# Two-layer diffusion trunk with expert-choice experts: last expert's rows added on the chip, another order in the ranking of layer 0, accumulated rows read in halves, and a hold on the expert weights

## What is computed

```python
def ec_moe(x, w_router, w_gate, w_up, w_down):
    cap = EC_CAPACITY * t // N_EXPERTS            # 64 latent rows, 16 context rows
    aff = jax.nn.softmax(logits, axis=1)
    gate, idx = lax.top_k(aff, cap)
    xs = jax.vmap(lambda xb, ib: xb[ib])(x, idx)
    hid = jax.nn.silu(xs @ w_gate) * (xs @ w_up)  # per expert, 1024 -> 512
    y = (hid @ w_down) * gate[..., None]          # per expert, 512 -> 1024
    return zeros.at[idx].add(y)

for layer in range(2):
    x = x + g1 * mixer(rms_norm(x, norm1) * (1 + sc1) + sh1)
    h = rms_norm(x, norm2) * (1 + sc2) + sh2
    x = x + g2 * ec_moe(h, ...)
y = rms_norm(x, final_norm)
```

## Time and profile before

| what | value |
|---|---|
| median of 3 runs | 1420.3 us (1416.61 to 1423.88) |
| the profiled execution | 1421.51 us, its span 1418.9 us |
| busy in the span: PE, PEld | 1264.6 us (89%), 916.2 us (65%) |
| busy: DVE, ACT, POOL | 872.5 us (61%), 734.3 us (52%), 215.8 us (15%) |
| DMA moved | 323.18 MB, mean 228 GB/s |
| chain that ended last | PE 71%, DMA 10%, DVE 9%, ACT 8%, issue 2% |
| mean granted TensorE clock | 0.945 of full |

### The profile page before, as it was taken

One profiled execution on the slowest core, in us unless ns is written; L12 is line 12 of the kernel. 1 busy time (PEld: TensorE's weight loads), 2 busy tenths in 40 slices (PEclk: granted clock), 3 DMA queues, 4 the chain that ended last, 5 costly groups with the idle time before them and its releaser, 6 DMA issues.

```text
span 1418.9 us, 18135 instructions
## 1 busy us (share of the span) xinstructions
PE 1264.6 (89%) x7524; PEld 916.2 (65%) x7524; DVE 872.5 (61%) x1005; ACT 734.3 (52%) x866; POOL 215.8 (15%) x126
## 2 busy tenths in 40 slices
PE   5899988898479999999689998999985899999991
PEld 3796756795256666666369994567954566666660
DVE  3713457424658888888274352454255699999993
ACT  3522137513547777778254114554145677777763
POOL 3000000020102222211120000000201033333320
PEclk9997799999889999999799999799998899999996
DMA  9721073004699999999793322002146999999985
GB/s 358 221 77 32 32 254 118 1 30 178 243 331 358 383 379 377 377 383 398 251 282 119 89 75 77 1 1 76 45 178 220 369 399 379 379 384 385 379 326 167
DMA packets 99047, 323.18 MB, mean 228 GB/s; under 512 B 6368, under 2 KB 30143, under 8 KB 82583
## 3 DMA queue, kind: packets, MB, share of 16 engines
q1 hardware_dynamic: 87360, 283.54, 53.2%
q0 software_dynamic: 9152, 30.53, 8.2%
q10 hardware_dynamic: 2454, 7.96, 1.5%
HBM read 298.20 MB, written 23.81 MB: 227 GB/s over the span
## 4 chain that ended last, share of the span: by engine, by line
PE 71%; DMA 10%; DVE 9%; ACT 8%; issue 2%; SPq 0%; ACTq 0%; DVEq 0%; POOLq 0%
PE psum L869 67%; ACT arena L1669 3%; DMA stage<-in_w_mod 2%; DVE arena L2119 2%; DVE w_lo L1841 2%; DMA arena<-in_moe_w_up 2%; DMA h_hi<-h_dram,arena 1%; DMA stage<-in_moe_w_gate 1%; DMA acc_dram<-arena 1%; PE psum L1349 1%; DMA arena<-acc_dram 1%; DVE arena L1879 1%; DMA arena<-in_ev_w_in 1%; DVE h_lo L1841 1%; ACT w_hi L1735 1%
## 5 line engine op out<-in xcount | busy, mean ns | idle before, releaser
L869 PE MATMUL psum<-w_hi,h_hi 128*80 128x512 f32 (+1 forms) x848 | 329.9, 389 | 12.5 <-DVE h_lo L1841 10.5
L1841 DVE TENSOR_TENSOR w_lo<-stage,w_hi 128x2048 fp32r<-128x2048 f32 (+1 forms) x120 | 270.9, 2270 | 89.6 <-ACT w_hi L1448 56.0
L869 PE MATMUL psum<-w_hi,h_lo 128*80 128x512 f32 (+1 forms) x848 | 325.9, 384 | 0.0
L869 PE MATMUL psum<-w_lo,h_hi 128*80 128x512 f32 (+1 forms) x848 | 325.7, 384 | 0.0
L869 PE MATMUL psum<-h_hi,w_hi 128*128 128x320 f32 x672 | 211.3, 314 | 6.9 <-DVE h_lo L1891 6.8
L1735 ACT ACTIVATE w_hi<-stage 128x2048 fp32r<-128x2048 f32 x98 | 186.7, 1915 | 44.3 <-PE psum L869 34.9
L869 PE MATMUL psum<-h_hi,w_lo 128*128 128x320 f32 x672 | 209.2, 311 | 0.0
L869 PE MATMUL psum<-h_lo,w_hi 128*128 128x320 f32 x672 | 209.2, 311 | 0.0
L1841 DVE TENSOR_TENSOR w_lo<-arena,w_hi 128x2048 fp32r<-128x2048 f32 x75 | 171.4, 2288 | 37.4 <-ACT w_hi L1735 36.9
L869 PEld LDWEIGHTS psum<-w_hi,h_hi 128*80 128x80 f32 (+1 forms) x848 | 129.8, 153 | 86.8 <-issue 14.8
L837 POOL DMA_INDIRECT acc_dram<-arena x32 | 120.6, 3770 | 427.2 <-ACT arena L1772 229.3
(11 more groups left out here) (236 smaller groups left out, 1296.0 us busy)
## 6 DMA issues: line engine op xcount, KB each, us to landing
stage<-in_w_mod SPq DMA_DIRECT2D x48, 1024.0 KB, 7.6
stage<-in_moe_w_up SPq DMA_DIRECT2D x35, 1024.0 KB, 14.7
stage<-in_moe_w_down SPq DMA_DIRECT2D x32, 1024.0 KB, 14.5
stage<-in_moe_w_gate SPq DMA_DIRECT2D x31, 1024.0 KB, 13.7
arena<-in_moe_w_gate SPq DMA_DIRECT2D x28, 1024.0 KB, 14.2
arena<-in_moe_w_up SPq DMA_DIRECT2D x24, 1024.0 KB, 15.3
arena<-in_moe_w_down SPq DMA_DIRECT2D x21, 1024.0 KB, 13.7
xT<-in_moe_w_down SPq DMA_DIRECT2D x11, 1024.0 KB, 19.5
```

What stands on the lines that cost most here:

```text
L869: return pe.matmul(o, w, x, start=first, stop=last, skip_group_check=True)
L1841: return nc.vector.tensor_tensor(dst, src, hi.bitcast(F32), ALU.subtract)
```

## The change

It has four parts.

1. **Hold.** In both layers SP waits, before the third weight block of the experts (expert 0's u0), until expert 0's rows are gathered. Before, this wait stood ahead of the eighth block in layer 0 and of the tenth in layer 1. One wait on the h stores is left out, since the gather implies it; the wait on the x stores in layer 1 stays.
2. **Ranked chunk first.** In layer 0 the `mod_rows` of the chunk of step "rank" moves ahead of the h transposes on PE, and its evacuation ahead of the h evacuations on ACT.
3. **Halves.** At the end of layer 0, ACT issues two reads (columns 0 to 511, 512 to 1023) in place of POOL's one; two of the four evacuations of step "acc" now stand behind that wait. PE transposes and DVE adds half by half.
4. **Last expert on the chip.** In layer 1, expert 15's rows aren't scattered. SP reads the tiles after expert 14's scatter. POOL counts 0 to 639 along 80 rows, DVE compares with the expert's token numbers, which makes an 80 x 640 one-hot matrix, and PE multiplies it (fp32, 10 matmuls of 512 columns) with the expert's rows. For tiles 0, 1 and 4 DVE adds the result to the tile read; for tiles 2 and 3, PE adds the tile in PSUM by four matmuls with the identity, and the norm works from PSUM. The tiles go in the order 0, 1, 4, 2, 3.

```diff
 def expert_piece(e, what):
...
+                    if m == 2:
+                        sp.wait_ge(gathered[0], 16 * (E // AHEAD * L + 1))
                     if m < SLOTS + len(lent_places):
...
                             filled(sp, (L, "h", NT - 1))
-                            if n in SUM_PLACES:
-                                sp.wait_ge(h_out[NT - 1], 16 * (L + 1))
-                            elif L == LAYERS - 1:
+                            if n in OUT_PLACES and L == LAYERS - 1:
                                 sp.wait_ge(x_stored, 16 * NT)
...
-            sp.wait_ge(scattered, 16 * E * LAYERS)
-            for t in range(NT):
-                sp.dma_start(acc_out[t], acc_dram[LAYERS - 1][P * t:P * t + P, :]).then_inc(acc_out_in[t], 16)
+            sp.wait_ge(scattered, 16 * (E * LAYERS - 1))
+            for t in TAIL_ORDER:
+                sp.dma_start(acc_last[t], acc_dram[LAYERS - 1][P * t:P * t + P, :]).then_inc(acc_out_in[t], 16)
...
 # pool
-                for e in range(E):
+                for e in range(E if L < LAYERS - 1 else E - 1):
...
-                pool.wait_ge(scattered, 16 * E * (L + 1))
-                if L < LAYERS - 1:
-                    pool.dma_start(xtok, acc_dram[L].rearrange("(t p) d -> p t d", p=P)).then_inc(acc_in, 16)
+                if L == LAYERS - 1:
+                    pool.wait_ge(lo_ready, moe_q[L] + piece_number(E - 1, "d0") + 1)
+                    pool.iota(one_hot, [[1, T]], base=0, channel_multiplier=0, allow_small_or_imprecise_dtypes=True).then_inc(token_numbers, 1)
...
 # tensor
+                if L == 0:
+                    mod_rows(ranked[0])
                 for t in range(NT):
...
+                if L == LAYERS - 1:
+                    pe.wait_ge(one_hot_ready, 1)
+                    pe.wait_ge(y_ready, n0 + E)
+                    for t in TAIL_ORDER:
+                        if t == 3:
+                            pe.wait_ge(x_added, 1)
...
+                            ins = mm(psum[:, TAIL_BANKS[t] + b, :], one_hot[rows, P * t:P * t + P], ysb[(E - 1) % 2][rows, cols_b],
+                                     True, t not in ADDED_BY_PE)
+                        if t in ADDED_BY_PE:
+                            pe.wait_ge(acc_out_in[t], 16)
+                            for b in range(2):
+                                ins = mm(psum[:, TAIL_BANKS[t] + b, :], ident, acc_last[t][:, FF * b:FF * b + FF], False, True)
...
-                    pe.wait_ge(acc_in, 16)
-                    to_features((L, "moe"), xtok)
+                    for b in range(2):
+                        pe.wait_ge(acc_in[b], 16)
...
 # scalar
-                    modulation("acc")
+                    modulation("acc", slice(0, 2))
+                    act.wait_ge(scattered, 16 * E * (L + 1))
+                    rows = acc_dram[L].rearrange("(t p) d -> p t d", p=P)
+                    for b in range(2):
+                        act.dma_start(xtok[:, :, FF * b:FF * b + FF], rows[:, :, FF * b:FF * b + FF]).then_inc(acc_in[b], 16)
+                    modulation("acc", slice(2, None))
...
 # vector
+                    nc.vector.tensor_scalar(one_hot, one_hot, last_slots, None, ALU.is_equal).then_inc(one_hot_ready, 1)
                 rows_out(E - 1)
...
+                nc.vector.tensor_tensor(x, psum[:, TAIL_BANKS[t]:TAIL_BANKS[t] + 2, :], x, ALU.add).then_inc(x_added, 1)
```

More of the change, by code:

```diff
@@ L267, in plan_psum @@
         p.add((L, "aff"), [4], "act"), p.add((L, "aff ctx"), [5], "act")
+        if L == 0:
+            p.add(("mod rows", ranked[0]), [6], "act")
         for t in range(NT):
@@ L271, in plan_psum @@
         for c in ranked:
-            p.add(("mod rows", c), [6], "act"), p.add(("mod turned", c), [6], "dve", in_order=False)
+            if L > 0:
+                p.add(("mod rows", c), [6], "act")
+            p.add(("mod turned", c), [6], "dve", in_order=False)
         for c in last:
@@ L287, in plan_psum @@
         mod("acc")
-        one((L, "moe", "ctx0"), "dve"), one((L, "moe", "ctx1"), "dve")
-        for k in range(KD):
-            one((L, "moe", k), "dve")
+        for b in range(2):
+            one((L, "moe", f"ctx{b}"), "dve")
+            for k in range(4 * b, 4 * b + 4):
+                one((L, "moe", k), "dve")
     return p
@@ L581, in trunk @@
         hid_step = sem("hid_step")
-        scattered, acc_in = sem("scattered"), sem("acc_in")
+        scattered, acc_in = sem("scattered"), [sem(f"acc_in{b}") for b in range(2)]
         dve_step = sem("dve_step")
+        token_numbers, one_hot_ready, last_added = (sem(n) for n in ("token_numbers", "one_hot_ready", "last_added"))
         def filled(eng, name):
@@ L662, in trunk, with summed_rows @@
         moe_q = [piece[(L, "moe", 0)]["q"] for L in range(LAYERS)]
+        def summed_rows(t):
+            if t not in ADDED_BY_PE:
+                return acc_last[t]
+            return psum[:, TAIL_BANKS[t]:TAIL_BANKS[t] + 2, :]
         block = ctx.enter_context(nc.Block())
@@ L1716, in _ @@
                 evacuate((L, "aff ctx"), work_ctx[:, 0:NC], bank((L, "aff ctx"))[CTX_ROW:RANKED, 0:NC])
+                if L == 0:
+                    modulation((L, "rank"))
                 for t in range(NT):
@@ L1816, in root_out_of @@
                 nc.scalar.activation(root_out[:, t:t + 1], root_out[:, t:t + 1], ACT.Exp, scale=-0.5).then_inc(root_done, 1)
-            for t in range(NT):
-                act.wait_ge(acc_out_in[t], 16)
-                nc.scalar.activation(x_out[t], acc_out[t], ACT.Square, accum_out=squares_out[:, t:t + 1]).then_inc(x_squared, 1)
-                if t:
-                    root_out_of(t - 1)
+            for n, t in enumerate(TAIL_ORDER):
+                if t in ADDED_BY_PE:
+                    act.wait_ge(last_added, n + 1)
+                else:
+                    act.wait_ge(x_added, n + 1)
+                src = summed_rows(t)
+                dst = y_rows[t].rearrange("p (b n) -> p b n", b=2) if t in ADDED_BY_PE else y_rows[t]
+                nc.scalar.activation(dst, src, ACT.Square, accum_out=squares_out[:, t:t + 1]).then_inc(x_squared, 1)
+                if n:
+                    root_out_of(n - 1)
             root_out_of(NT - 1)
@@ L2286, in _ @@
                 expert_split(E - 1, "d1")
+                if L == LAYERS - 1:
+                    then(nc.vector.tensor_copy(last_slots, slots[:, E - 1:E]))
+                    dve.wait_ge(token_numbers, 1)
+                    nc.vector.tensor_scalar(one_hot, one_hot, last_slots, None, ALU.is_equal).then_inc(one_hot_ready, 1)
                 rows_out(E - 1)
@@ L2299, in _ @@
                 newton(mean, root)
-                nc.vector.scalar_tensor_tensor(x_out[t], acc_out[t], root, gain_rows, ALU.mult, ALU.mult).then_inc(y_done, 1)
+                dst, gain = y_rows[t], gain_rows
+                if t in ADDED_BY_PE:
+                    dst, gain = (x.rearrange("p (b n) -> p b n", b=2) for x in (dst, gain))
+                    dve.wait_ge(last_added, n + 1)
+                nc.vector.scalar_tensor_tensor(dst, summed_rows(t), root, gain, ALU.mult, ALU.mult).then_inc(y_done, 1)
+            add_last(0)
+            add_last(1)
+            mean_of(0)
+            add_last(2)
+            mean_of(1)
+            scale_rows(0)
+            mean_of(2)
+            scale_rows(1)
+            mean_of(3)
+            scale_rows(2)
+            mean_of(4)
+            scale_rows(3)
+            scale_rows(4)
 _OUTS = {"y_prompt": (1, NC, D), "y_sample": (1, NL, D), "new_k": (1, 1, KV, NC, HD), "new_v": (1, 1, KV, NC, HD),
```

70 lines of the change are left out of this document (53 added, 17 removed).

## The result

The changed kernel takes 1431.4 us (median of 4 runs, 1429.6 to 1433.4) against 1419.9 before; the ratio is 1.0083, 95% interval 1.0065 to 1.0101. The forecast was 1414.6, with a range of 1405 to 1421. The profiled execution took 1432.5 us, its span is 1430.3.

What follows compares the result with a forecast made beforehand. PE and the weight stream's DMA are both full, so PE computes as fast as weights come. Layer 0's ranking +1.0, halves −2.0, layer 1's ranking +1.0, tail −5.7 sum to −5.7: median 1420.3 to 1414.6 us, range 1405 to 1421.

Steps and rivals of the forecast that it cites:

- by the row the matmuls start at 2.4 GHz and the tail gives −5.7: Tail: 14 fp32 matmuls at full clock take 12.2 us, PE resting only about 1.3 us before; −5.7 us.
- the rival of 1.2 GHz: Tail: its matmuls run at 1.2 GHz throughout, +6.5 in place of −5.7, so 1426.8 us; chance 0.06.
- a clock of 0.5: Tail: a granted clock of 0.5 under the new matmuls, listed among the signs that the forecast is wrong.
- Layer 1's hold: Layer 1's ranking: gather issued near 1087.3, landing at 1091.2; 0.4 to 1.2 us more idle DMA, taken as +1.0.
- Layer 0's hold: Layer 0's ranking: gather of 3.9 us, weight stream falls back by 0.6 to 2.1 us, taken as +1.0.
- a trap: Layer 0, ACT: u0 is split ahead of the gathered rows, so the rows wait for a load that waited for them.
- I take −2.0: Layer 0's end: reading the accumulated rows in two halves lets PE finish its transposes earlier; bounds 0 and 4, −2.0 us.
- The ranked chunk first: Layer 0's ranking: modulation matmuls ahead of 40 transposes free stage slots earlier; h evacuations come 1.9 us later.
- Slow gathers: Both rankings: the gather's 9.3 us are its own, not the load's; +6.4 in each layer, 1425.4 us; chance 0.13.
- PE's start decides: Both layers: weights catch up as PE starts earlier; layer 0 −2.6, layer 1 −4, 1406.0 us; chance 0.20.
- The hold does nothing net: Both layers: what is lost is regained exactly and both end where they did; −7.7, 1412.6 us; chance 0.14.
- The rule on DMA issue: Layer 0's end: all issuers share 16 DMA engines, so moving the read from POOL to ACT brings nothing; sum unchanged.

Runs made afterwards that it cites:

- the mended tail alone: The kernel before with only the last expert added on the chip, its one-hot matmuls at 128 rows: 1413.0 us (12 runs), ratio 0.9958.

## Why the prediction was wrong

The change took 11.5 us where a gain of 5.7 was forecast. In steps of medians: the tail's matmuls at 64 rows rather than full height, 8.1; the hold, 6.1; what is left of the change without both is a gain of 3.2 (1417.2 against 1420.5 beside it). That these give 11.0 is no proof, since the steps follow on one another. The 3.2 are less than the 6 to 9 that the tail gains alone at full height, so some 2 to 5 us go with the ranked chunk and the halves beside it. The profiles point to the chunk, but the intervals of the two ratios (0.9975 and 0.9958) overlap, and this part stays open.

- **The tail: the main failure, at the step "by the row the matmuls start at 2.4 GHz and the tail gives −5.7".** They did start there, but the step took the clock to depend on PE's rest alone and gave the rival of 1.2 GHz a chance of 0.06, "against it: the short rest". The rest isn't what let it fall: with it filled, the clock fell too, if later; with full height and the same rest, it didn't. Matmuls of 64 rows, back to back, did not hold the higher clock; nor did those of 10 and 8 rows at 127.40 in the trace before, a row that the prediction had not looked at. The row used for the duration, the norm's sums at 0.87 each, was of full height (128*128), and so was right for full-height matmuls only. At full height the −5.7 hold (6 to 9 measured). The rival had the place right, but not the cause, and its price was too high: 12.2 us for the lower clock throughout, where 7.6 were lost (19.8 against 12.2). That its 1426.8 came nearer than the forecast owes something to luck, as the other terms missed too. The prediction had named a clock of 0.5 here as a sign of being wrong.
- **Layer 1's hold: right mechanism, wrong size.** The prediction counted idle DMA time, 0.4 to 1.2 us more, and took +1.0; measured 4.3 by the medians, 6.2 by the ratios. Of the miss, 2 us are the gather: issued at 1091.84, which is as early as forecast, given the lateness of some 4.5 us by then, it let SP go at 1097.77, after 5.9 us instead of 3.9; the x stores ran beside it from 1094.55 on. For the rest, the traces point to the prediction's having looked at the stream's end alone. Before, u0 and u1 were sent at 1079.53, now at 1097.77. Experts 0 and 1 need the held blocks one after another, and ACT waited 16 us for four of them, where in the trace before it had no such wait.
- **Layer 0's hold: about right.** +1.0 forecast, 1.8 by medians and nothing by the ratios. The quiet gather was 4.5 (3.9 forecast), the last store landed at 381.8 (380.5). u0 took 8.6 us, not the 6.0 that the prediction gave it with the gathers beside it; seven blocks were let go within 4 us, which is the likely reason. The order on ACT, called a trap, cost 0.8 by medians, not clear of noise; the rows and u0 are both needed soon. The fall of the DMA share from 0.95 to 0.90, which the prediction had counted as the hold's, comes without the hold as well.
- **The halves: the step "I take −2.0" failed.** The sums did come 3 us or more earlier, but the prediction stopped its chain at the sums. What is late next was the load of the following modulation chunk, which SP sends only after the rows. Measured: nothing (ratio 1.0003).
- **The ranked chunk first:** no price of its own in the sum, only 1.9 us on the h stores. In the time none is shown (ratio 1.0008); in the profiles layer 0 loses 2 to 3 us with it.
- **The rivals.** Slow gathers: no, they were quick in both layers. PE's start decides: no. The hold does nothing net: true of layer 0 within the noise, not of layer 1.
- **The rule on DMA issue** (the Trainium skill, Trainium Kernel Development and Optimization, Key Constraints): this case agrees. Two reads from ACT took 11.2 us in the chain of the halves alone, where POOL's one took 11.32.

## What to carry to other kernels

Holding back a stream that later sets the pace costs the DMA time left idle, and more where the held blocks are needed one by one right after. If a hold is wanted, give quiet to the stores alone and let the stream go while the gather is under way: that was 11 us better here than holding until the rows were gathered, 5 better than no hold (only just told apart), and no better than the mended tail alone. Before work is moved to TensorE, look at the height of its matmuls as well as at its rests, and look in the trace for other low ones with PE busy; zero rows up to the full 128 cost nothing here and kept the clock. When a stage is made quicker, follow the chain past it to the next wait before its gain is counted.

## What was not expected of the hardware

Fp32 matmuls that fill 64 of 128 rows (one pair 16) let the granted clock fall from 2.4 to 1.2 GHz while PE was busy without a gap, in nine profiles of nine, and the clock rose again within a us of the full-height identity matmuls that followed (0.50 up to 1418, 0.86 from 1418 to 1420); the same matmuls over 128 rows, those added with zero weights, ran at 2.4 GHz in eight profiles of eight (14 matmuls in 12.3 against 19.8 us). A quiet gather took 4.5 us, and 5.9 with the x stores beside its end, where a loaded one takes 9.3; in the eight us up to 1094, in which layer 1's gather was prepared and issued, four fifths of the DMA time stood idle.
